# Sorting the 32 experts of a mixture-of-experts layer by row count, and computing 15 of them as 64-row float32 blocks on two column halves of TensorE

## The reference

```python
def hier_moe(h, rg_w, rg_b, re_w, re_b, w1, w3, w2):
    ...
    e_p, e_idx = lax.top_k(jax.nn.softmax(sel, axis=-1), TOP_K)       # TOP_K = 2
    weights = g_p * e_p / jnp.sum(e_p, axis=-1, keepdims=True)
    expert_id = g_idx * EXPERTS_PER_GROUP + e_idx
    ...
    def expert_block(args):
        xb, e = args
        return (jax.nn.silu(xb @ w1[e]) * (xb @ w3[e])) @ w2[e]
    ...
    y = jax.ops.segment_sum(out * row_w[:, None], row_tok, num_segments=t + 1)
```

## Time and profile before

| | us |
|---|---|
| median of 3 runs | 1857.88 |
| lowest and highest run | 1856.87, 1858.93 |
| span of the profiled execution, first to last instruction | 1850.9 |
| TensorE busy in the span | 1695.2 (92%) |
| VectorE busy | 1216.4 (66%) |
| ScalarE busy | 906.9 (49%) |
| HBM traffic in the span | 342.79 MB read, 70.33 MB written |

### The profile page before, as it was taken

How to read it: one execution, slowest core, us unless ns; L and a number is a source line. 1 busy time by engine, 2 the same in 40 slices (tenths; PEclk the granted TensorE clock), 3 DMA queues, 4 the chain that set the end, 5 groups by cost and what they waited for, 6 DMA issues and landing times. The chain is left out here.

```text
span 1850.9 us, 31750 instructions
## 1 busy us (share of the span) xinstructions
PE 1695.2 (92%) x12198; PEld 1386.1 (75%) x12198; DVE 1216.4 (66%) x1549; ACT 906.9 (49%) x1315; POOL 456.5 (25%) x644
## 2 busy tenths in 40 slices
PE   5999999899989977999899999278999999999986
PEld 5688888887878855778788788167888888888862
DVE  5655455420117756878454554668999999999975
ACT  2641111132127754545321322257888888888861
POOL 1100011200020005677420011113433423334315
PEclk9999999999989988989889999589999999999998
DMA  9368666431435712322544232638999999999966
GB/s 330 125 204 299 226 205 230 169 121 41 120 94 133 166 36 61 74 56 43 191 143 144 59 123 93 279 144 323 390 383 382 392 381 388 379 375 389 378 258 271
DMA packets 150799, 397.96 MB, mean 215 GB/s; under 512 B 51297, under 2 KB 67712, under 8 KB 129184
## 3 DMA queue, kind: packets, MB, share of 16 engines
q1 hardware_dynamic: 119200, 328.77, 49.1%
q0 software_dynamic: 16736, 41.34, 6.2%
q10 hardware_dynamic: 14752, 26.29, 3.8%
HBM read 342.79 MB, written 70.33 MB: 223 GB/s over the span
## 5 line engine op out<-in xcount | busy, mean ns | idle before, releaser
L2777 DVE TENSOR_TENSOR ex_w_r<-w,ex_w_r 128x1024 fp32r<-128x1024 f32 x384 | 451.7, 1220 | 22.6 <-ACT ex_w_r L2706 12.4
L2706 ACT ACTIVATE ex_w_r<-w 128x1024 fp32r<-128x1024 f32 x384 | 404.3, 1063 | 88.4 <-PE psum L2634 88.4
L2632 PE MATMUL psum<-ex_w_r,ex_x_t 128*128 128x512 f32 x512 | 203.9, 398 | 4.0 <-DVE ex_x_t L2777 2.4
L2634 PE MATMUL psum<-ex_w_r,ex_x_t 128*128 128x512 f32 x512 | 201.6, 394 | 0.0
L2633 PE MATMUL psum<-ex_w_r,ex_x_t 128*128 128x512 f32 x512 | 201.3, 393 | 0.0
L555 ACT ACTIVATE stage<-psum 128x512 f32<-128x512 f32 (+1 forms) x72 | 41.4, 574 | 301.9 <-PE psum L157 192.1
L2582 POOL COPY ex_idx<-row_pair 128x1 int32 (+1 forms) x32 | 34.3, 1072 | 374.4 <-ACT ex_y L2706 374.4
L155 PE MATMUL psum<-w_even,h_hi 128*128 128x512 f32 (+1 forms) x320 | 119.1, 372 | 4.8 <-ACT stage L555 4.8
L156 PE MATMUL psum<-w_even,h_hi 128*128 128x512 f32 (+1 forms) x320 | 118.7, 371 | 0.0
L157 PE MATMUL psum<-w_even,h_lo 128*128 128x512 f32 (+1 forms) x320 | 118.7, 371 | 0.0
L2632 PEld LDWEIGHTS psum<-ex_w_r,ex_x_t 128*128 128x128 f32 x512 | 97.2, 190 | 24.1 <-DVE ex_x_t L2777 2.8
(11 more groups left out here) (442 smaller groups left out, 3942.7 us busy)
## 6 DMA issues: line engine op xcount, KB each, us to landing
w<-in_exp_w SPq DMA_DIRECT2D x128, 1024.0 KB, 15.4
w<-in_exp_w SPq DMA_DIRECT2D x32, 2048.0 KB, 9.1
w_ring<-in_ada_w SPq DMA_DIRECT2D x12, 2048.0 KB, 11.2
w_ring<-in_w_in SPq DMA_DIRECT2D x10, 2048.0 KB, 11.3
qk<-stage_r ACTq DMA_DIRECT2D x16, 512.0 KB, 7.7
gates<-stage ACTq DMA_DIRECT2D x32, 256.0 KB, 2.0
bl_gates<-gates SPq DMA_DIRECT2D x8, 1024.0 KB, 4.9
w<-pair_rows SPq DMA_DIRECT2D x16, 512.0 KB, 9.4
```

Of the source, the lines that this page charges most:

```text
L2632: nc.tensor.matmul(out, lhs[0], hi, start=first, stop=False)
L2634: return nc.tensor.matmul(out, lhs[1], hi, start=False, stop=last)
L2706: return nc.scalar.activation(out, src, ACT.Copy)
L2777: return nc.vector.tensor_tensor(out, whole, high.bitcast(F32), ALU.subtract)
```

## The change

Experts 0 and 1 stay first (their weights are loaded ahead). The other 30 are ranked by row count on the chip: the 15 with the most rows get blocks of 128 rows with parity 0 (as expert 0 has; expert 1 is the one 128-row block of parity 1), and the 15 with the fewest get blocks of 64 rows with parity 1. Rows beyond a block's room go to overflow blocks of parity 0, each of which adds a pair. A 64-row block splits nothing: its matmuls take the raw weights as float32, 64 rows (columns of the stationary operand) at a time, and two of them, one for each half of the output columns, write the two halves of the partitions of one bank. Its up product is 8 x 2 matmuls with 512 moving columns, its down product 4 x 2, and it has 2 transposes of hidden values in place of 4. Its raw buffers are free only when its matmuls have read them (`small_up_used`, `small_down_used`). Its w2 is laid out in another order, and its result is scattered as 128 half rows of 2 KB (`row_half`). The order of the slots is unchanged: large and small alternate. `slots` waits for `blocks` after the third slot, no longer ahead of the first; SP now waits for it ahead of its first `load_next`. The tables are 64 columns wide where they were 48. The small block's banks are 5 (up) and 6 (down). The core of the diff:

```diff
-BLOCKS = E + OVERFLOW_BLOCKS
+PAIRS_MAX = E // 2 + OVERFLOW_BLOCKS
+BLOCKS = 2 * PAIRS_MAX
+SMALL = P // 2
+BIG_FIRST = E // 2 + 1
...
+        total = run[:, :, TT - 1]
+
+        link(stt(out=size[:], in0=total, scalar=float(E), in1=size_bias[:], op0=ALU.mult, op1=ALU.add))
+        link(tt(larger[:], size[:].unsqueeze(1).to_broadcast([P, E, E]), size[:].unsqueeze(2).to_broadcast([P, E, E]), ALU.is_gt))
+        link(red(order[:], larger[:], AX.X, ALU.add))
+        link(ts(is_small[:], order[:], float(BIG_FIRST) - 0.5, None, ALU.is_gt))
+        link(stt(out=column[:], in0=is_small[:], scalar=float(PAIRS_MAX - E // 2 + 1), in1=order[:], op0=ALU.mult, op1=ALU.add))
+        link(tt(column[:], column[:], column_bias[:], ALU.add))
+        link(ts(room[:], is_small[:], float(SMALL - P), float(P), ALU.mult, ALU.add))
+
+        link(tt(beyond[:], total, room[:], ALU.subtract))
+        link(tt(more, beyond[:].unsqueeze(2).to_broadcast([P, E, TT]), steps[:].unsqueeze(1).to_broadcast([P, E, TT]), ALU.is_gt))
+        link(red(extra[:], more, AX.X, ALU.add))
+        link(nc.vector.tensor_tensor_scan(extra_end[:], ones_e[:], extra[:], 0.0, ALU.mult, ALU.add))
+
+        link(tt(over_row[:], extra_end[:], extra[:], ALU.subtract))
+        link(ts(over_row[:], over_row[:], float(P), float(E // 2 * P), ALU.mult, ALU.add))
+        link(tt(over_row[:], over_row[:], room[:], ALU.subtract))
+        link(stt(out=diff[:], in0=column[:], scalar=float(P), in1=over_row[:], op0=ALU.mult, op1=ALU.subtract))
...
+        link(tt(row[:], tmp[:], be(room[:], E), ALU.is_lt))
+        link(tt(row[:], row[:], be(diff[:], E), ALU.mult))
...
+        link(ts(holder[:, 0, :], column[:], own[:, 0:1], None, ALU.is_equal))
+        link(tt(holder[:, 0, :], holder[:, 0, :], iota_e[:], ALU.mult))
+        link(ts(holder[:, 1, :], extra_end[:], own[:, 1:2], None, ALU.is_le))
+        link(red(held[:], holder[:], AX.X, ALU.add))
+        link(ts(held[:, 1:2], held[:, 1:2], float(E - 1), own[:, 2:3], ALU.min, ALU.mult))
+        tt(held[:, 0:1], held[:, 0:1], held[:, 1:2], ALU.add).then_inc(sig("held"), 1)
...
+        dve.wait_ge(sig("halves_flipped"), 1)
+        link(nc.vector.tensor_copy(half_f[:], bank[4][:, 0:PAIRS_MAX]))
+        link(stt(out=half_taken[:], in0=half_f[:], scalar=0.0, in1=free_row[:, 0:PAIRS_MAX], op0=ALU.is_equal, op1=ALU.mult))
+        link(tt(half_f[:], half_f[:], half_taken[:], ALU.add))
+        link(ts(half_f[:], half_f[:], 2.0, own[:, 3:4], ALU.mult, ALU.add))
+        nc.vector.tensor_copy(keep["row_half"][:], half_f[:]).then_inc(sig("row_half"), 1)
...
+    if small:
+        src = src.rearrange("(h p k) n -> p h k n", h=2, k=FE // P // 2)
+        sp.dma_start(keep["w2"][:, par].rearrange("p (h k) n -> p h k n", h=2), src).then_inc(sig(f"w2_in{par}"), 16)
...
+        def small(blk):
+
+            return blk[0] == 1 and not (isinstance(blk[1], int) and blk[1] == 0)
...
-                    sp.wait_ge(sig("up_lo"), up_count((par, i), HALF_K * (q + 1)))
+                    if small(blk):
+                        sp.wait_ge(sig("small_up_used"), 2 * i + (q - 1))
+                    else:
+                        sp.wait_ge(sig("up_lo"), up_count(blk, HALF_K * (q + 1)))
                     load_up(nc, sp, sig, keep, ins, par, q, e)
-                sp.wait_ge(sig("down_lo"), down_count((par, i), FK))
-                load_down(nc, sp, sig, keep, ins, par, e)
-
+                if small(blk):
+                    sp.wait_ge(sig("small_down_used"), i)
+                else:
+                    sp.wait_ge(sig("down_lo"), down_count(blk, FK))
+                load_down(nc, sp, sig, keep, ins, par, e, small_next)
...
+                if small((par, pair)):
+                    at = index(1, keep["row_half"], P, (par, pair), pair)
+                    pool.indirect_dma_start(dram["pair_rows"].rearrange("r (a n) -> (r a) n", a=2), at, y[:, par, 0:NC5], None,
+                                            bounds_check=4 * S - 1, oob_is_err=False).then_inc(sig(f"y_out{par}"), 16)
...
+            def up_small(blk):
+
+                par, pair = blk
+                for k in range(KT):
+                    if k % HALF_K == 0:
+                        pe.wait_ge(sig(f"w13_in{par}{k // HALF_K}"), 32 * (pair + 1))
+                    for h in range(2):
+                        last = nc.tensor.matmul(bank[5][h * SMALL:(h + 1) * SMALL, :].rearrange("p (j n) -> p j n", j=2), x_s[:, k, :],
+                                                w13[:, par, :, k, h * FE // 2:(h + 1) * FE // 2], start=(k == 0), stop=(k == KT - 1))
+                    if k % HALF_K == HALF_K - 1:
+                        last.then_inc(sig("small_up_used"), 1)
...
+                if small(blk):
+                    pe.wait_ge(sig(f"w2_in{par}"), 16 * (pair + 1))
+                    for k in range(FK):
+                        for half in range(2):
+                            last = nc.tensor.matmul(bank[first_bank][half * SMALL:(half + 1) * SMALL, :], hid_s[:, k % 2, k // 2, :],
+                                                    w2[:, par, k, half * NC5:(half + 1) * NC5], start=(k == 0), stop=(k == FK - 1))
+                    last.then_inc(sig("small_down_used"), 1)
...
+                if small(blk):
+
+                    pe.wait_ge(sig(f"hidden{par}"), pair)
+                    up_small(blk)
+                else:
+                    if before and small(before):
+
+                        pe.wait_ge(sig(f"hidden{par}"), pair)
+                    elif before:
+                        pe.wait_ge(sig(f"hidden{before[0]}"), before[1] + 1)
+                    up_big(blk)
...
+                    act.wait_ge(sig("down_used"), down_count(before, 0))
+                    down_hi(before, lambda u: (sig("up_used"), up_count(before, u + RING + 1)))
+                    act.wait_ge(sig("small_up_used"), 2 * pair)
+                    nc.scalar.activation(sigm[:, 0:FE // 2], bank[5][:, 0:FE // 2], ACT.Sigmoid).then_inc(sig(f"sigm{par}"), 1)
+                else:
+                    up_hi(blk, range(RING, KT), lambda u: (sig("up_used"), up_count(blk, u - RING + 1)))
+                    if before and not small(before):
+                        down_hi(before, lambda u: (sig("up_used"), up_count(blk, u + RING + 1)))
...
+                if behind:
+                    x_hi(behind)
+                    if not small(behind):
+                        if before:
+                            up_hi(behind, range(RING), lambda u: (sig("down_used"), down_count(before, u + 1)))
+                        else:
+                            up_hi(behind, range(RING), lambda u: (sig("up_used"), up_count(blk, u + RING + 1)))
```

More of the change, by code:

```diff
@@ L2276, in routing @@
         idx = sb("rt_idx", [P, TT])
+        size_bias = sb("rt_size_bias", [P, E])
+        column_bias = sb("rt_column_bias", [P, E])
+        steps = sb("rt_steps", [P, TT])
+        own = sb("rt_own", [P, 4])
+        size = sb("rt_size", [P, E])
+        larger = sb("rt_larger", [P, E, E])
+        order = sb("rt_order", [P, E])
+        is_small = sb("rt_is_small", [P, E])
+        room = sb("rt_room", [P, E])
+        column = sb("rt_column", [P, E])
+        beyond = sb("rt_beyond", [P, E])
         extra = sb("rt_extra", [P, E])
@@ L2325, in route_pool @@
         for par in range(2):
[L2326 removed]
+            first = par * PAIRS_MAX
+            link(nc.gpsimd.tensor_copy(idx[:, 0, par:par + 1], keep["row_token"][:, first:first + 1]))
             nc.gpsimd.tensor_tensor(keep["ex_spare"][:], const["neghalf"][:, 0:1], const["neghalf"][:, 0:1], ALU.mult)
@@ L2643, in flip_x, with up_big @@
                 last.then_inc(sig(f"x_flipped{blk[0]}"), 1)
+            def up_big(blk):
+                for k in range(KT):
+                    pe.wait_ge(sig("up_lo"), up_count(blk, k + 1))
+                    for j in range(2):
+                        last = product(bank[2 + j], [x_t[:, blk[0], i, k, :] for i in range(2)], k,
+                                       slice(j * FE, (j + 1) * FE), k == 0, k == KT - 1)
+                    last.then_inc(sig("up_used"), 1)
+            def up_small(blk):
+                par, pair = blk
+                for k in range(KT):
+                    if k % HALF_K == 0:
[5 more added lines that the diff above has]
+                        last.then_inc(sig("small_up_used"), 1)
@@ L2681, in slot @@
                 if before:
-                    pe.wait_ge(sig(f"hid_lo{before[0]}"), before[1] + 1)
-                for k in range(FK):
+                    pe.wait_ge(sig(f"hid_t{before[0]}"), before[1] + 1)
+                for k in range(2 if small(blk) else FK):
                     last = nc.tensor.transpose(bank[4][:, k * P:(k + 1) * P], hidden[:, k * P:(k + 1) * P], ident[:])
@@ L2797, in slot @@
                 if not before:
-                    x_lo(*blk)
-                up_lo(blk, range(RING, KT))
-                if before:
+                    x_lo(blk)
```

(11 more changed lines are left out.)

229 lines of the change are left out of this document (122 added, 107 removed).

## The result

| | before | after |
|---|---|---|
| median, us (4 runs each) | 1857.38 | 1833.18 |
| lowest and highest | 1844.64, 1858.93 | 1825.97, 1836.98 |
| ratio, 95% interval | | 0.9889 [0.9843, 0.9936] |
| span of the profiled run | 1850.9 | 1834.9 |
| step of a pair (every second w2 load) | 35.48 | 34.79 |

The account below looks back on a forecast made before the run. TensorE was taken as the bound (35.48 us a pair), with DMA next at 33.9. Pair 15 starting 23.2 us earlier and 6.7 off the tail cut the span from 1850.9 to 1821; plus 7.0 gave 1828.0, range 1806 to 1850.

Parts of the forecast that it names:

- Full overlap of the halves: Small block on TensorE: paired matmuls on the two column halves run at once, up product 6.9 us, down product 3.4.
- Rivals (2): Small block: halves do not overlap with 512 columns, pair 39.4 us, TensorE the bound again, time 1918; chance 0.07.
- (3): Small block: weight loads of 137 ns stand between the matmuls, pair 35.7 us, time near 1863; chance 0.04.
- Routing 4.5 us longer: Routing ahead of the expert loop: added operations cost 6.4 us and dropped ones save 1.9, a net 4.5 us.
- The first pairs: Start of the expert loop: pair 2 begins at 1294.1 and, with no DMA backlog yet, pair 3 at 1325.
- TensorE's pair of 29.1 us: Expert loop: TensorE's work for one large and one small block takes 29.1 us in place of 35.48.
- The step of 33.9 us: Expert loop: DMA sets each pair's time, 13.63 MB at 402 GB/s, 33.9 us, never running dry.
- rival (1): Expert loop: in-order wait for small w2, with low clock, leaves DMA dry 1.5 us; period near 35.6, time 1848; chance 0.24.
- The tail: End of the expert loop: from pair 15's start to the last down product's end 36.0 us, 6.7 less than before.
- 7.0 us around the span: Whole kernel: the median time lies 7.0 us above the profiled span, so this was added to the span of 1821.
- Rival (4): Expert loop: DMA does better, near 423 GB/s, time 1808; chance 0.07.
- Rival (5): Expert blocks: the split is not 17 and 15, an overflow adds a pair of some 34 us, time 1862; chance 0.01.

Follow-up runs that it names:

- x2_order: The changed kernel with SP's wait for the small w2 moved behind the large block's first two loads, inside the loop: 1830.82 us, ratio 0.9871.
- x4_delay: The changed kernel with ten filler matmuls (2.3 us) ahead of the small down product: 1856.65 us.
- x10_order_delay: x2_order with the ten filler matmuls of x4_delay ahead of the small down product: 1840.6 us.
- x6_floor: x2_order with only the first of the three products in each large block: 1813.76 us.
- x5_serial: The changed kernel with, in the small products, all matmuls of one column half ahead of all of the other: 1873.84 us.
- x9_sort_only: The routing and expert order of the change, with every block computed as in the kernel before: 1855.93 us, ratio 1.0028.
- x7_floor_w2: x6_floor with the w2 of small blocks read in the layout of before: 1825.5 us.
- x3_warm: The changed kernel with twelve filler matmuls (2.7 us) ahead of each large up product: 1825.24 us, ratio 0.9863.
- x8_order_all_warm: x2_order plus the filler of x3_warm, with loads in the order their buffers come free from the first pair on: 1826.82 us, ratio 0.9877.
- x12_order_warm: x2_order with the twelve filler matmuls of x3_warm ahead of each large up product: 1831.8 us, ratio 0.9892.

## Why the prediction was right, and which of its steps were not

The forecast of 1828.0 us was met within 5.2 us. Its main mechanism holds: TensorE's work falls below what DMA needs, and the pair then follows DMA. That it came so near is in part luck: the step was mis-sized by some 11 us in all, and an error in another term took half of that back. Step by step:

- **Full overlap of the halves**: right. 7.09 and 3.65 us were measured for 6.9 and 3.4. Rivals (2) and (3) fall: records follow after 0.22 us although each loads its own weights. The weight loads (mean 137 ns) have these rows on the page:

```profile
L2748 PE MATMUL psum<-w,ex_x_s 128*64 128x512 f32 x480 | 106.3, 595 | 0.0
...
L2748 PEld LDWEIGHTS psum<-w,ex_x_s 128*64 128x64 f32 x480 | 33.1, 137 | 62.5 <-issue 62.5
```

  A record lasts 595 ns (by the profile, which models the ends of matmuls) and follows the one before after 220 on average. Two records, one on each half, take the 0.43 us that one takes by itself in the earlier trace rows; their two loads of 137 ns would add 0.27 if they stood between them. The rule of the Trainium skill (TensorE: Matmul & The Clock Gate, What overlaps and what doesn't), that a load overlaps matmuls only where the row group differs, does not describe this case.
- **Routing 4.5 us longer**: right. From the router's result on VectorE to `row_token` it was 28.08 us (1172.13 to 1200.21) and is 32.62 (1176.50 to 1209.12). The working was a little less exact than its sum: it takes off 1.9 us where its own item is 1.7.
- **The first pairs**: pair 2 was forecast at 1294.1 and began at 1295.3, or 1290.9 after taking off 4.4 us by which this execution was late ahead of routing. Pair 3 was forecast at 1325 and began at 1328.8, or 1324.4 so corrected: the pair between was 2.6 us longer than forecast, and both errors cancel.
- **TensorE's pair of 29.1 us**: 31.8 were measured (34.79 less 3.0 idle). Of the difference 1.6 is the low clock at the start of the large up product, which takes 12.6 us for 11.0. It was named in the prediction and not in the sum.
- **The step of 33.9 us**: too short by 0.9, and the only term of weight. Over the 12 pairs from pair 3 on it puts pair 15 at 1747.4, or 1743.0 so corrected, for 1731.8 forecast. The step that failed is "a backlog of some 2.6 us stands, and DMA never runs dry": it does, for 1.6 us a pair. The low clock after each wait (0.50 at 1506 to 1507.5) makes up 1.6 of the 2.0 us by which the release is later, T + 17.3 for T + 15.3, and the backlog is used up; the step is 17.3 + 17.2. This is rival (1), true in its mechanism and in its 1.5 us of dry queue; its period of 35.6 was 0.8 us too long. The other assumption, 402 GB/s as what the mix always gives, came from dividing 386 by a share of 0.96. That leaves out that slow stretches have a full share, and that they can grow. With the dry stretch removed (x2_order), the early pairs go faster (409) and the late ones slower (385).
- **The tail**: 35.8 us, from 1747.36 to the end of the last down product (1783.1), for 36.0 forecast.
- **7.0 us around the span**: wrong. In the executions that have both numbers, time and span differ by 1.8 us in nearly all (1836.66 and 1834.9) and by 3.3 at most. The rest was the difference between executions: the profiled one of before was quicker than the three runs beside it, and ordinary among later ones, of which 12, 11 and 23 have medians of 1852.36, 1850.57 and 1849.42. This error of +5 us hid half of the error in the step. The gain itself was forecast at 29.9 us and is 20 to 23 between the stages (627.7, and 607.5 or 604.8), 24 between the medians.
- **Rival (4)**, near 423 GB/s: no. Seven slices of ten do stand at 420; the rest is lost. **Rival (5)**: there were 17 and 15 blocks, as counted.

Shown by runs: that the wait's place lets TensorE's delay through (x4_delay, x10_order_delay), that DMA sets the step once the wait is moved (x6_floor), that the halves need turns (x5_serial), that neither the sorting nor the layout of w2 matters (x9_sort_only, x7_floor_w2). Seen in one execution only: that the full clock takes 0.3 to 0.4 us off a pair (x3_warm). Open: why late pairs of the reordered kernels lose more to slow stretches than early ones, and what slows DMA while the rows of a 64-row block are gathered. The intervals of x2_order, x3_warm, x8_order_all_warm and x12_order_warm overlap one another and that of the kernel after; x3_warm has the lowest median (1825.24), and none is shown to be better.

## What to carry to other kernels

When a change takes an engine below the next limit, work out the next limit as bytes at the undisturbed rate plus each stretch in which the queue is dry or slow, and read those stretches from the GB/s slices of one period; an average rate divided by its share hides both. When a buffer is held longer than before, look at what is queued behind its wait: here 1.6 of 2.3 us of a later release came back in every pair, and almost nothing once the wait was moved behind the loads that did not need it. When two limits lie close together, removing one gains little: here no more than 0.4 us a pair, and nothing that the time shows.

## What the runs showed of the hardware that was not expected

- While the rows of a 64-row block are gathered there are some 3 us in which the DMA engines are busy and move only 280 to 290 GB/s; it costs 0.8 us a pair, with or without stores. The gather of a 128-row block in the same pair has no such stretch (410 to 429 GB/s).
- The DMA share goes to 1.05 and above in short windows (1.08 at 1497.0), so that 0.98 on average still held 1.6 us of dry time a pair.
- Float32 matmuls on the two column halves overlap fully when they alternate (7.09 us for 32 records, 0.22 each), and only around the change of halves when they don't (12.29 us for 32).
- With twelve matmuls of no use ahead of the large product the pair was 0.3 to 0.4 us shorter and the granted clock 1.00 in place of 0.94, in one execution; the time shows no gain that is clear of its scatter.
